# Hybrid decoder trunk: shift and scale loaded ahead of the heads in 1 MB pieces, the output gates' modulation computed in portions inside the heads

## The reference, cut to what matters

```python
mod = jax.nn.silu(c) @ w_ada + b_ada                 # w_ada: 2048 x 6144 per layer
shift, scale, gate = jnp.split(mod, 3, axis=-1)
h = _rmsnorm(x, g_norm) * (1.0 + scale[:, None, :]) + shift[:, None, :]
cols = jnp.split(h @ w_in, ...)                      # 16 heads of four 128-column tiles
...                                                  # the heads (HGRN2, mLSTM, retention) give o
o = o.astype(x.dtype) * jax.nn.silu(z)
y = x + gate[:, None, :] * (o @ w_out)
```

## Time and profile before

| | |
|---|---|
| time, median of 3 executions | 2620.52 us (2617.19 to 2623.05) |
| the profiled execution | 2616.45 us, its span 2614.6 us |
| granted TensorE clock, mean | 0.977 of full speed |
| TensorE busy | 2418.6 us, 93% of the span |
| VectorE, ScalarE, GpSimd busy | 1257.1, 760.9, 936.5 us |
| moved by DMA | 340.82 MB |

### The profile page before, as it was taken

The page is one execution under the profiler, slowest core; times in us unless marked ns, Lnnn a source line. Parts: engine busy times, 40 slices in busy tenths (PEclk is TensorE's granted clock), DMA queues, the critical chain, the costliest instruction groups (busy, mean ns, idle before and its releaser), DMA issues.

```text
span 2614.6 us, 49278 instructions
## 1 busy us (share of the span) xinstructions
PE 2418.6 (93%) x20866; PEld 2180.5 (83%) x20866; DVE 1257.1 (48%) x2416; ACT 760.9 (29%) x1191; POOL 936.5 (36%) x668
## 2 busy tenths in 40 slices
PE   3775999979999999999999899997999999999898
PEld 2114999959999999997777799996999999999898
DVE  6004555536776743342111655553767763344434
ACT  2002323223333333341111423323333333234111
POOL 0001533413443434454222433431433434445442
PEclk9997999989999999999999899998999999999999
DMA  5996333323333343327998633332333343333442
GB/s 173 321 314 203 98 99 83 84 74 83 94 89 99 99 116 104 104 80 233 289 298 260 184 98 84 83 99 59 90 93 106 86 117 103 104 95 82 132 116 88
DMA packets 473558, 340.82 MB, mean 130 GB/s; under 512 B 17781, under 2 KB 416593, under 8 KB 472017
## 3 DMA queue, kind: packets, MB, share of 16 engines
q1 hardware_dynamic: 473338, 337.67, 44.6%
HBM read 305.78 MB, written 32.04 MB: 129 GB/s over the span
## 4 chain that ended last, share of the span: by engine, by line
PE 75%; DVE 8%; DMA 8%; ACT 4%; POOL 2%; DVEq 2%; issue 1%; SPq 1%; ACTq 0%
PE pj L565 59%; DMA raw<-in_w_ada 4%; PE mx L571 2%; DMA raw<-in_w_out 2%; POOL wlo L533 2%; PE mx L795 1%; PE mx L630 1%; ACT whi L948 1%; PE pj L645 1%; PE mx L574 1%; PE mx L809 1%; PE mx L705 1%; PE pj L683 1%; PE mx L821 1%; ACT zw L948 1%
## 5 line engine op out<-in xcount | busy, mean ns | idle before, releaser
L533 POOL TENSOR_TENSOR wlo<-raw,whi 128x512 fp32r<-128x512 f32 x632 | 892.3, 1443 | 1581.4 <-ACT whi L948 1581.4
L565 PE MATMUL pj<-hh,whi 128*128 128x260 f32 x5056 | 1049.9, 289 | 47.4 <-POOL wlo L533 40.7
L565 PE MATMUL pj<-hh,wlo 128*128 128x260 f32 x5056 | 1021.1, 284 | 0.0
L565 PE MATMUL pj<-hl,whi 128*128 128x260 f32 x5056 | 1020.5, 283 | 0.0
L565 PEld LDWEIGHTS pj<-hh,whi 128*128 128x128 f32 x5056 | 781.1, 190 | 123.7 <-issue 102.2
L565 PEld LDWEIGHTS pj<-hl,whi 128*128 128x128 f32 x5056 | 783.7, 189 | 0.0
L565 PEld LDWEIGHTS pj<-hh,wlo 128*128 128x128 f32 x5056 | 782.7, 189 | 0.0
L948 ACT ACTIVATE whi<-raw 128x2048 fp32r<-128x2048 f32 x158 | 302.7, 1916 | 331.0 <-DMA raw<-in_w_out 188.4
L948 ACT ACTIVATE xv<-pj 128x260 f32<-128x260 f32 x192 | 66.2, 384 | 416.6 <-PE pj L565 399.5
L1188 DVE SCALAR_TENSOR_TENSOR o<-pj,mod,t 128x260 f32<-128x260 f32 x64 | 28.0, 480 | 315.5 <-PE pj L565 315.5
L645 PE MATMUL pj<-raw,sct 128*32 128x512 f32 x384 | 100.1, 635 | 45.9 <-DMA raw<-in_w_ada 45.7
(11 more groups left out here) (252 smaller groups left out, 2211.4 us busy)
## 6 DMA issues: line engine op xcount, KB each, us to landing
raw<-in_w_in SPq DMA_DIRECT2D x256, 512.0 KB, 5.2
raw<-in_w_ada SPq DMA_DIRECT2D x96, 512.0 KB, 5.3
raw<-in_w_out SPq DMA_DIRECT2D x64, 512.0 KB, 5.9
lev<-in_w_ada SPq DMA_DIRECT2D x58, 512.0 KB, 5.0
xv<-in_w_ada SPq DMA_DIRECT2D x38, 512.0 KB, 5.3
out<-ss SPq DMA_DIRECT2D x32, 512.0 KB
y_kept<-o SPq DMA_DIRECT2D x2, 4160.0 KB, 12.0
t<-y_kept SPq DMA_DIRECT2D x32, 260.0 KB, 5.4
```

Of the source, the lines that this page charges most:

```text
L533: last = e.tensor_tensor(wlo[:, par, cs], w[:, cs], high_of(t)[:, cs].bitcast(F32), ALU.subtract)
L565: last = e.matmul(pj[:, 2 * par + b, 0:HALF], w[:, par, kb * P:(kb + 1) * P], x[:, kb, b * HALF:(b + 1) * HALF], start=(kb == 0 and m == 0 ...
```

## The change

- The pieces ahead of the heads hold only shift and scale of layer 0: 32 pieces of 1 MB. The first 16 are one kb by the 2048 columns of shift (8 KB rows), the next 8 are two kb by the first half of scale, the last 8 by its second half (4 KB rows). They go to twelve slots (`piece_slot`): `raw`, the room of `whi` and `wlo`, and room that x's rows or h take at other times. TensorE multiplies a piece into four groups of 32 partitions.
- x is no longer saved at the start but after the loads of head 0's tiles t+2 and t+3; the first two tiles are loaded after piece 17, the level mask after piece 11.
- silu(c) is computed on 128 partitions of 144 columns, from the turned c, by logarithm and exponential.
- h is made in two halves of eight kb, in both layers; in layer 0 each half follows the half of scale that it needs, and the last five pieces are multiplied between the first kb of the first two tiles.
- The gate third of both layers is made inside the layer's own heads from `FIRST_ML` on: 32 portions of two kb by 512 columns (two DMAs of 256 KB, 2 KB rows, into `gate_a` and `gate_b`), three a head, after tile 1, after the fourth eighth of tile 2 and after tile 2. SyncE loads a portion once TensorE has used the one before. VectorE adds the portions up in `gate_sum` (`gate_sums`), TensorE turns the sums at the start of the out phase.
- In the out phase of layer 0 the modulation of layer 1 is 32 pairs of pieces and 8 calls of `ada_columns`; the small parameters of layer 1 are loaded and taken there as well.

```diff
-ADA_GROUPS = 3 * D // ADA_N
+ADA_GROUPS = 2 * D // ADA_N
...
+FIRST_PIECES = 32
+SESSIONS = 32
...
-            return pair * 6 // 5
+            return pair * 9 // 5
...
-                for n in range(0 if l else ADA_GROUPS):
-                    for s in range(ADA_PIECES):
-                        piece = n * ADA_PIECES + s
-                        if piece >= RAW:
-                            e.wait_ge(ada_used, piece - RAW + 1)
-                        e.dma_start(raw[:, s % RAW, :].rearrange("p (k n) -> p k n", k=ADA_K),
-                                    wa[:, ADA_K * s:ADA_K * (s + 1), n * ADA_N:(n + 1) * ADA_N]).then_inc(ada_in[s % RAW], 16)
...
+            def first_piece(p):
+
+                at = piece_at[piece_slot[p]]
+                earlier = [x for x in range(p) if piece_slot[x] == piece_slot[p]]
+                if earlier:
+                    e.wait_ge(piece_used, earlier[-1] + 1)
+                elif piece_slot[p] in (6, 7, 8, 9):
+                    e.wait_ge(xt_ready, KB)
+                wa = w_ada[0].rearrange("(k p) n -> p k n", p=P)
+                if p < KB:
+                    src, dst = wa[:, p, 0:D], at
+                else:
+                    b, k = divmod(p - KB, KB // 2)
+                    src = wa[:, 2 * k:2 * k + 2, D + b * D // 2:D + (b + 1) * D // 2]
+                    dst = at.rearrange("p (k n) -> p k n", k=2)
+                e.dma_start(dst, src).then_inc(piece_in[piece_slot[p]], 16)
...
+            for p in range(FIRST_PIECES):
+                first_piece(p)
+                if p == 5:
+                    params(0)
+                if p == 11:
+                    e.dma_start(levf[:, 0:LEVELS * 128], lm_d).then_inc(lm_in, 16)
+                if p == 17:
+                    e.wait_ge(piece_used, 2)
+                    first_tiles(0)
...
-                    e.wait_ge(out_added, l * KB)
-                e.dma_start(y_kept[l], o[:].rearrange("p k t -> p (k t)")).then_inc(y_saved, 16)
...
                 e.dma_start(conv_s[l, :, 0:PAD - 1, :], st_conv[l, :, 1:PAD, :]).then_inc(stored, 16)
-                e.wait_ge(ada_used, ADA_GROUPS * ADA_PIECES)
...
                     load(t + 2, 0, wi[:, :, i * HD + cols[2]:(i + 1) * HD + cols[2]])
                     load(t + 3, 1, wi[:, :, COL_Z + slot * HD:COL_Z + (slot + 1) * HD])
+                    if h == 0:
+                        if l == 0:
+                            e.wait_ge(xt_taken, KB)
+                            e.wait_ge(sct_taken, 1)
+                        else:
+                            e.wait_ge(out_added, l * KB)
+                        e.dma_start(y_kept[l], o[:].rearrange("p k t -> p (k t)")).then_inc(y_saved, 16)
+
...
+                            return
+                        if session == 0:
+                            e.wait_ge(prm_taken, 2 * (l + 1))
+                            e.wait_ge(head_done, l * NH + FIRST_ML + 1)
+                        e.wait_ge(gate_used, l * SESSIONS + session)
+                        block, k = divmod(session, 8)
+                        for j, at in enumerate((gate_a, gate_b)):
+                            e.dma_start(at, w_ada[l].rearrange("(k p) n -> p k n", p=P)
+                                        [:, 2 * k + j, 2 * D + 512 * block:2 * D + 512 * (block + 1)]).then_inc(gate_in[j], 16)
+
+                    gate_load(0)
...
                             load(t + 4 + j, j, wo[:, :, j * P:(j + 1) * P])
+                        if j == 0:
+                            gate_load(1)
+                            gate_load(2)
...
+                def first_piece(p):
+
+                    e.wait_ge(piece_in[piece_slot[p]], 16 * (loads_of(p) + 1))
+                    at = piece_at[piece_slot[p]]
+                    if p < KB:
+                        w = at.rearrange("p (c j n) -> p j c n", j=4, n=P)
+                        for j in range(4):
+                            last = e.matmul(mx[32 * j:32 * j + 32, 0, :].rearrange("p (c n) -> p c n", n=P), sct[:, p, :], w[:, j],
+                                            start=(p == 0), stop=(p == KB - 1))
...
+                        for x in range(2):
+                            w = at.rearrange("p (k c j n) -> p k j c n", k=2, j=4, n=P)[:, x]
+                            for j in range(4):
+                                last = e.matmul(mx[32 * j:32 * j + 32, 1 - b, 0:2 * P].rearrange("p (c n) -> p c n", n=P),
+                                                sct[:, 2 * k + x, :], w[:, j], start=(k == 0 and x == 0), stop=(k == 7 and x == 1))
+                    last.then_inc(piece_used, 1)
...
+                def gate_session(h, x):
+
+                    session = session_of(h, x)
+                    if session >= SESSIONS:
+                        return
+                    e.wait_ge(head_done, l * NH + h + 1)
+                    for i, at in enumerate((gate_a, gate_b)):
+                        e.wait_ge(gate_in[i], 16 * (l * SESSIONS + session + 1))
+                        for j in range(4):
+                            last = e.matmul(mx[32 * j:32 * j + 32, 3, x * P:(x + 1) * P], sct[:, 2 * (session % 8) + i, :],
+                                            at[:, j * P:(j + 1) * P], start=(i == 0), stop=(i == 1))
+                    last.then_inc(gate_used, 1)
...
                 if l == 0:
-                    ada_columns(ADA_GROUPS - 1, (t1, t2), 0, 0)
-                if l:
+                    for p in range(27):
+                        first_piece(p)
+                        if p == 9:
+                            params()
+                        if p == 12:
+                            norm(0)
+                        if p == 17:
+                            block_columns(0)
+                        if p == 24:
+                            block_columns(1)
+                else:
                     norm(l)
...
                 for kb in range(KB):
+                    if kb % 8 == 0:
+                        e.wait_ge(hs_ready, 2 * l + kb // 8 + 1)
                     e.wait_ge(h_ready, l * KB + kb + 1)
                     last = [quarter(par, kb, parts=KB) for par in range(2)]
+                    if l == 0 and kb < 5:
+                        first_piece(27 + kb)
+                    if l == 0 and kb == 6:
+                        block_columns(2)
                 last[0].then_inc(tile_done, 1)
                 last[1].then_inc(tile_done, 1)
...
+                    if h >= FIRST_ML:
+                        for j, part, x in ((0, 7, 0), (1, 3, 1), (1, 7, 2)):
+                            own[j][part] = own[j].get(part, ()) + (lambda x=x: gate_session(h, x),)
...
                 e.wait_ge(head_done, (l + 1) * NH + 1)
+                for c in range(4):
+                    last = tr(mx[:, 3, c * P:(c + 1) * P], gate_sum[:, c, :], P)
+                last.then_inc(gate_tr, 1)
                 for n in range(KB):
                     for part in range(0 if n > 1 else 3, 4):
                         out_part(n, part)
+                        if l == 0 and (n, part) == (10, 3):
+                            e.wait_ge(gate_ready, 1)
+                            params_next()
...
-            e.wait_ge(x_in, 64)
-            act(e_row, crow, ACT.Exp, scale=-1.0).then_inc(c_exp, 1)
...
+            c_cols, c_log = t1[:, 0:9 * KB], t2[:, 0:9 * KB]
+            act(c_cols, mx[:, 2, 0:9 * KB], ACT.Copy)
+            act(c_log, mx[:, 2, 0:9 * KB], ACT.Abs)
+            e.drain()
+            act(c_log, c_log, ACT.Exp, scale=-1.0)
+            e.drain()
+            act(c_log, c_log, ACT.Ln, bias=1.0).then_inc(silu_log, 1)
+            e.wait_ge(silu_sig, 1)
+            act(c_log, c_log, ACT.Exp).then_inc(silu_exp, 1)
...
+
+                e.wait_ge(piece_used, KB + b * KB // 2)
+                if b == 0:
+                    act(zw[:, 0:T], mx[:, 0, :], ACT.Copy).then_inc(block_taken, 1)
+                else:
+                    act(z[:, 2 * (b - 1) * P:2 * b * P], mx[:, 2 - b, 0:2 * P], ACT.Copy).then_inc(block_taken, 1)
...
-                if l:
+                if l == 0:
+                    e.wait_ge(prm_tr, 1)
+                    params(1)
+                    norm(0)
+                    block_take(0)
+                    for j in range(2):
+                        high(j, 1, j, False)
+                    block_take(1)
+                else:
                     for j in range(2):
                         high(l * TILES + j, l * TILES // 2 + 1, j)
...
+                    if l == 0 and kb == 7:
+                        block_take(2)
                     if kb == 9:
                         high(l * TILES + 2, l * TILES // 2 + 2, 0, False)
...
-            e.wait_ge(c_exp, 1)
-            ts(e_row, e_row, 1.0, None, A_)
-            e.drain()
-            e.reciprocal(e_row, e_row)
-            e.drain()
-            tt(crow, crow, e_row, M).then_inc(silu_c, 1)
...
+            e.wait_ge(silu_log, 1)
+            c_cols, c_log = t1[:, 0:9 * KB], t2[:, 0:9 * KB]
```

(54 more changed lines are left out.)

221 lines of the change are left out of this document (113 added, 108 removed).

## The result

The changed kernel takes 2516.73 us (median of 4 runs, 2516.26 to 2520.64) against 2619.17 us before (2617.19 to 2623.05): a ratio of 0.961, 95% interval 0.9594 to 0.9627. Forecast were 2518 us and a range of 2502 to 2543.

A forecast was written before the change was run, and what follows sets the result against it. It took the start to be bound by waits for `w_ada` transfers, the heads by TensorE. Terms -121 + 38 - 23 + 2 + 1 = -103 us gave 2513.5 us, plus 4 for the runs' median: 2518 us, range 2502 to 2543.

The forecast's parts named there:

- Part A: Start, up to the third tile of layer 0: it starts at 142.5 instead of 263.7 us, -121 us.
- the 3 us of share shortfall: Start, transfers of pieces: DMA engines at 97% share rather than full cost 3 us more.
- the 43 us for scale: Start: the 16 pieces of scale, 16.8 MB in 4 KB rows, move at 390 GB/s and take 43 us.
- the 4.5 us there for the lower clock: Start, kb 0 to 4 with pieces 27 to 31: TensorE's clock at 1.2 GHz for the first 5 us adds 4.5 us.
- Part B: Gate portions in the heads: 64 portions at 0.59 us of TensorE each, loads and sums hidden, +38 us.
- Part C: Out phase of layer 0: 20 fewer insertions at 1.17 us, 0.18 of it in line 565, -23 us.
- Part D: Layer 1's start: VectorE makes h in two halves, +2 us on the path.
- Part E: Each out phase: turning the gate sums, +1 us.
- Rival 1: Start: 1 MB pieces move at the old 343 GB/s whatever their rows, +12 to +15 us, 2531 us; chance 0.23.
- Rival 2: Heads: portions land a little late, TensorE stands 0.5 to 1 us at 42 portions, +20 to +40 us; chance 0.10.
- Rival 3: Heads: portions land very late, TensorE waits 3.4 us at each, +143 us, 2661 us, slower than before; chance 0.02.
- Rival 4: Start: h and pieces interleave better or the clock stays at 2.4 GHz, up to 10 us less, 2508 us; chance 0.10.

The follow-up runs named there:

- the six starts: Six profiled executions with the changed kernel's own start (the changed kernel and edits of later stages only); the third tile starts at a mean of 134.9 us.
- experiment 1: Changed kernel with the third tile's weights loaded right behind the last piece, ahead of the small loads: 2516.1 us.
- experiment 2: Changed kernel with the third tile's weights loaded first and the second half of scale turned after kb 5 instead of kb 6: 2512.4 us.
- experiment 10: Changed kernel with only the second half of scale turned sooner, after kb 5 instead of kb 6: 2519.8 us.
- experiment 5: Changed kernel with each gate portion's matmuls issued twice in layer 1: 2532.7 us.
- experiment 11: Changed kernel with the w_out loads issued sooner in layer 0's out phase (4n - 9 instead of 4n - 6): 2508.6 us.

## Why the prediction was right

Its time is off by 1 us, but that is in part luck: errors of both signs cancel, and even their sum is 7 us off in the traces (-95.7 us for a forecast of -103). The medians lie closer to the forecast only since the changed kernel's profiled execution is the slowest of its four.

- **Part A** (-121, measured -126.6; -128.8 against the mean of the six starts). The first tile starts at 96.5 instead of 100.5 us: piece 26 has landed at 94.5, not 99.5. The mis-sized terms are the 3 us of share shortfall (the engines were at 101%) and the 43 us for scale, which took 16 x 2.56 = 41. From piece 26 to h of kb 8 it was 23.1 us for 25.2. The five kb with pieces took 13.1 us of it (96.49 to 109.60) for 16.7: the 4.5 us there for the lower clock did not come, and they were also twice what 5 us at 2.6 instead of 1.45 us a kb can lose (2.2 us). The lower clock came later, behind kb 9, so that from h of kb 8 to the third tile it was 19.5 us for 17.6. (The terms behind piece 26 add up to 40.3 us, not 40.5.) The two waits behind VectorE's start were forecast, one by its length (3 us), and are what experiments 1, 2 and 10 remove.
- **Part B** (+38, measured +47.9). The portion's own 0.57 us was forecast at 0.59; what failed is that its price ended there. The 0.18 us of restart, which I had counted for each insertion in Part C, was left out here: 64 x 0.17 = 11 us. That loads and sums are hidden held: TensorE waited 0.5 us for the loads, and for VectorE in the eleven heads of layer 0 with portions 18.9 us, where it was 19.0 before. The Trainium skill (TensorEngine Tiling (Array Packing), Key Properties) says that a change of tiling mode drains TensorE. What experiment 5 measured fits that, since half of a portion's price is not its columns; no run here changes the mode by itself, so that the drain is this half is not shown.
- **Part C** (-23, measured -16.1). The pairs taken out did give what was forecast of them: their line's busy time fell from 53.4 to 36.3 us. The 0.18 us times 20 did not come: what I had read as restart in line 565's 10.7 us more in layer 0 was partly something else. In the changed kernel it is 185.7 against 174.3 us, 11.4 us, for only 40 insertions; with the w_out loads in time (experiment 11) 180.5 against 174.3, 6.2 us, 0.16 for each of 40. The other 5 us go with the lower clock behind stands (0.97 of full speed over the phase for 0.99 in experiment 11). This is the term that the prediction lacked: a late w_out load costs the stand (11.5 us idle for 9.4 before; the waits for `wlo` 8.4 for 5.5) and then clock (four places at about 0.8 for one). That they grew because the pairs taken out had covered the loads is argued, not shown; that the order of the loads makes them is shown by experiment 11.
- **Parts D and E** (+2 and +1, measured 0 and about 0): the change of layer takes 40.5 us in both (where the forecast 2 us went was not looked into), and the end and the last out phase together 0.8 us less.
- **Rival 1** fell: 410 GB/s, and 388 even in the old form. The Trainium skill (DMA: Bandwidth & Descriptors, Bandwidth) gives 341 GB/s for a DMA of 1 MB, measured on DMAs that GpSimd issued; the 410 GB/s here show that figure not to bound DMAs of SyncE that are queued behind each other. **Rivals 2 and 3** fell with the 0.5 us of waits for the portions. **Rival 4** came half true (5.4 of its up to 10 us, 7.6 against the mean start).

## What to carry to other kernels

Small pieces of work put into a stream of matmuls cost their insertion as much as their columns: price both, in every stage. Where a bound engine has work taken away, ask which loads that work may have covered, and where in the issuing queue they stand: here one number in the order of SyncE's DMAs was worth 14 us of a phase. And two waits in a row are to be removed together, since the first alone only lengthens the second.

## What the runs showed of the hardware that I had not expected

- The same start ended between 133.9 and 137.1 us in six executions. A stand of 3.18 us of TensorE was followed at once by pairs at the lower clock in some (0.72 to 0.77 us for the first) and not in others (0.48), with a clock of 0.68 to 0.92 from 120 to 128 us; after a stand of 1.75 us with none behind it the clock stayed at 1.00 in both executions that had it. So a stand costs its length and, by an estimate from these shares of 8 us, up to 0.6 to 2.6 us of clock.
- An issue of a tiny DMA (`gb`) held SyncE 3.8 to 7.5 us while pieces were still in flight; in the six executions with the same start it was over at 106.0 to 106.8 us, however early it began. With the weights' load ahead of it, the stand moved to that load (3.43 us in experiment 1) and to `gw` (4.26), and 2.44 us stayed at `gb`.
- 1 MB pieces moved at 410 GB/s with rows of 8 and of 4 KB, at 388 with 2 KB, whether as one DMA or as two.
